# Block inverses of the recurrent stage: VectorE's 32x32 transposition and level products 32 columns wide

## The chip, the core and the metric

The kernel runs on one core of one Trainium2 chip. The metric is device time in microseconds (us) for one launch, lower is better. TensorE (PE in the profile) multiplies matrices: it loads a stationary operand (PEld, a weight load) and streams a moving operand past it, into PSUM. VectorE (DVE), ScalarE (ACT) and GpSimd (POOL) work elementwise. Each engine runs its own instruction stream in order and waits for the others by semaphores.

## The reference

Two transformer-like blocks are computed one after the other for 512 tokens of 1024 channels. The first has a feed-forward network, a mixer of three branches and a second feed-forward network. The second has a bidirectional recurrence (RWKV-7), a neighbourhood attention, a merge, and a mixture of 16 experts. Only the recurrence bears on this case. It has 8 heads of 64 channels, two directions, first 256 context tokens and then 512 latent tokens:

```python
def rwkv_scan(s0, r, decay, k, v, kk, a, reverse, emit):
    def step(s, inp):
        w_t, k_t, v_t, kk_t, a_t = inp[:5]
        s_kk = jnp.einsum('bhvk,bhk->bhv', s, kk_t)
        s = (s * w_t[:, :, None, :]
             - s_kk[..., None] * (kk_t * a_t)[:, :, None, :]
             + v_t[..., None] * k_t[:, :, None, :])
        y = jnp.einsum('bhvk,bhk->bhv', s, inp[5]) if emit else None
        return s, y
...
    for d in range(2):
...
        s_c, yc_d = rwkv_scan(s0, r_c, w_c, kd_c, v_c, kk_c, a_c, rev, emit_ctx)
        w_x, kd_x, a_x = dir_x[d]
        _, yx_d = rwkv_scan(s_c, r_x, w_x, kd_x, v_x, kk_x, a_x, rev, True)
```

## The kernel before

**Chunks.** The recurrence is not run token by token. It goes over 12 chunks (`NCH`) of 64 tokens (`L`): chunks 0 to 3 are context and emit nothing, chunks 4 to 11 emit outputs (`emits`). Both directions are done together. A "tile" is 64x64; a chunk has 8 tiles of one kind (`ALL`): 4 for direction 0 (`LOW`), 4 for direction 1 (`HIGH`). Each tile holds two heads, one in partitions 0 to 63, one in 64 to 127. `tiles` (L1978) issues one matmul per head, so two per tile, all at L1983. A product `ALONG` keeps a head in its own half of partitions, one `ACROSS` lands in the other half.

**What a chunk needs.** Inside a chunk the delta rule needs the inverse X of a unit triangular 64x64 matrix per head and direction, made from the pair product A = kappa x b. The pair products are `AT` (transposed), `A`, `CT`, `R1`, `R2`, and the transposes `kT`, `bT`, `vt`, which are matmuls against the identity. The state products are G, U, Z and y. The `lora_pe` matmuls (L2019) make decays for the chunk after next.

**The inverse by levels.** `XX[c % 2]` holds X and its transpose XT side by side for each direction. ScalarE writes identities there (`unit`, L1908, 128x1024). VectorE then copies the neighbour elements of AT into XT and of A into X under a mask (`pair_XT`, `pair_X`, each a `copy_predicated`, L2273). From there five levels l = 1 to 5 join blocks of 2^l into blocks of 2^(l+1). Each level has four steps for each direction d:

- PE: Y = A times X, 4 tiles of 64 columns (`level_Y`).
- DVE: `Ym` = Y times the level's mask, 128x256 (`level_y`, L2291).
- PE: W = X times Ym into the X half of a PSUM bank, and its transpose into the XT half, 8 tiles (`level_W`); at level 5 only the transposed one, 4 tiles.
- DVE: XX += W, 128x512, at level 5 128x256 (`level_x`, L2299).

**The order.** It is written out by hand. On PE the loop over chunks interleaves each level product with another product that is ready (`beside`, tile by tile), such as the next chunk's pair products or the last chunk's state products; `alone` issues one kind only. On VectorE the loop puts other work between the masked products and the additions: the scaled keys of the next chunk after `level_y` of level 1, the decay logits of the chunk after next at level 2, `pair_XT` and a scan at level 3, `pair_X` after `level_x` of level 3, the state addition (L2305), the CT mask (L2286) and a key product at level 4, the state decay (L2311) and a scan before level 5. Every wait is on a semaphore whose value a table of names gives (`Marks`, `Steps`).

A "full" chunk window, as the prediction uses it, is one in which the next chunk emits and the chunk after next still needs its decays: 496 matmuls.

Of the kernel before, what the change touches and what calls it, by code (L numbers as in the profile page):

```python
# [14 lines left out]
P = 128  # L15
# [83 lines left out]
def hybrid_block_kernel(nc, stream, par, x_t, mod_w, c_rows, vbias, gate_w, masks, ctx_t, rpb, router_w, lora, experts, spill, gates_dram, xs_dram, ys_dram, out):  # L99
    ctx = ExitStack()  # L100
    with ctx:
# [447 lines left out]
        hz_ready = sem("hgrn_zeros")  # L549
# [4 lines left out]
        zero_ready = sem("zero_ready")  # L554
# [13 lines left out]
        def hgrn_pool(pool):  # L568
            pool.dma_start(vb, vbias).then_inc(vb_in, 16)
            pool.memset(zero_row[:, :], 0.0).then_inc(zero_ready, 1)  # L570
            pool.wait_ge(zero_ready, 1)
# [6 lines left out]
            pool.memset(ql, 0.0).then_inc(hz_ready, 1)  # L578
            pool.memset(kl, 0.0).then_inc(hz_ready, 1)
# [204 lines left out]
        def hgrn_dve(dve):  # L784
# [43 lines left out]
            def head(h):  # L828
# [13 lines left out]
                if h == 0:  # L842
                    dve.wait_ge(hz_ready, 2)
# [76 lines left out]
        l_zero = sem("lru_zeros")  # L920
# [6 lines left out]
        def lru_pool(pool):  # L927
            pool.wait_ge(hv.sem, hv.end(HEADS))
            pool.memset(lxp[:, 0:3], 0.0).then_inc(l_zero, 1)
            pool.memset(acc_odd[:, 0:1], 0.0).then_inc(l_zero, 1)  # L930
# [56 lines left out]
        def lru_act(act):  # L987
            s = la.sem
            act.sem_inc(s, la.base)
            act.wait_ge(l_zero, 2)  # L990
# [63 lines left out]
        def lru_dve(dve):  # L1054
            s = lv.sem
            dve.sem_inc(s, lv.base)
            dve.wait_ge(l_zero, 2)
# [689 lines left out]
        Ym, Gs, Us = take(W8, "a"), take(W8, "a"), take(W8, "a")  # L1747
        yacc = take(8 * 4 * L, "a").rearrange("p (c q v) -> p c q v", c=8, q=4)
# [24 lines left out]
        M_BANK = dict(vt=6, AT=4, A=5, CT=6, kT=4, bT=5, R1=6, R2=4)  # L1773
# [18 lines left out]
        pe_m = Marks("rwkv_pe_pairs", lambda c: ("AT", "A", "CT", "kT", "bT") + (("R1", "R2") if emits(c) else ()) + ("vt",))  # L1792
# [8 lines left out]
        dve_l = Marks("rwkv_dve_levels", lambda c: [f"{n}{l}{d}" for l in LV for n in ("ym", "x") for d in range(2)])  # L1801
# [7 lines left out]
        rz = sem("rwkv_zeros")  # L1809
# [18 lines left out]
        def rwkv_pool(pool):  # L1828
# [3 lines left out]
            pool.memset(st[0], 0.0).then_inc(rz, 1)  # L1832
            pool.memset(reset, 1.0).then_inc(rz, 1)
            pool.wait_ge(rz, 2)
            pool.memset(bd(reset)[:, :, 0:1], 0.0).then_inc(rz, 1)
# [44 lines left out]
        def rwkv_act(act):  # L1880
# [90 lines left out]
        def rwkv_pe(pe):  # L1971
# [6 lines left out]
            def tiles(n, bank, *terms, start=None, at=None):  # L1978
# [12 lines left out]
            ALL, LOW, HIGH = range(8), range(4), range(4, 8)  # L1991

# [39 lines left out]
            def pair_A(c):  # L2032
                if c:
                    W(act_m, c - 1, "bT")
                return lambda n: tiles(n, M_BANK["A"], (ACROSS, of(kap[c % 3]), of(bt)))

# [10 lines left out]
            def pair_bT(c):  # L2047
                W(dve_m, c, "X")
                return lambda n: tiles(n, M_BANK["bT"], (ACROSS, of(bt), eye))

# [14 lines left out]
            def level_Y(c, l, d):  # L2065
                if l == 1:
                    W(act_m, c, "AT")
                    W(dve_m, c, "X")
                    if c:
                        W(dve_l, c - 1, f"x5{d}")  # L2070
                else:
                    W(dve_l, c, f"x{l - 1}{d}")
                return lambda n: tiles(n, d, (ALONG, of(AT[c % 2]), X_of(c)), at=n % 4 * L)

            def level_W(c, l, d):
                W(dve_l, c, f"ym{l}{d}")

                def one(n):
# [58 lines left out]
            pe.wait_ge(rz, 3)  # L2137
            pe.wait_ge(kn_dve.sem, kn_dve.end(1))
            alone(pair_AT(0), ALL, pe_m)
            alone(pair_A(0), ALL, pe_m)  # L2140
# [4 lines left out]
            for c in range(NCH):  # L2145
# [9 lines left out]
                w = level_W(c, 1, 0)  # L2155
                beside(w, ALL, pe_l, pair_vt(c), ALL, pe_m)
                alone(level_W(c, 1, 1), ALL, pe_l)
# [4 lines left out]
                if more:  # L2162
                    beside(w, ALL, pe_l, pair_AT(n), ALL, pe_m)
                    w = level_W(c, 2, 1)
                    beside(w, ALL, pe_l, pair_A(n), ALL, pe_m)
                    level_Ys(c, 3, pair_CT(n), pe_m)
                else:
                    alone(w, ALL, pe_l)
                    alone(level_W(c, 2, 1), ALL, pe_l)
                    level_Ys(c, 3)  # L2170
                w = level_W(c, 3, 0)
                if last:
                    z = state_Z(s)
                    beside(w, ALL, pe_l, z, LOW)
                    w = level_W(c, 3, 1)
                    beside(w, ALL, pe_l, z, HIGH, pe_s)
                else:
                    alone(w, ALL, pe_l)
                    alone(level_W(c, 3, 1), ALL, pe_l)
# [5 lines left out]
                if y:  # L2185
                    beside(w, ALL, pe_l, state_y_old(s), ALL, pe_s)
                    alone(state_y_new(s), ALL, pe_s)
                else:
                    alone(w, ALL, pe_l)
                w = level_W(c, 4, 1)  # L2190
                if more:
                    beside(w, ALL, pe_l, pair_bT(n), ALL, pe_m)
                else:
                    alone(w, ALL, pe_l)
# [4 lines left out]
                if r:  # L2199
                    other = pair_R2(n)  # L2200
                    w = level_W(c, 5, 0)
                    beside(w, HIGH, pe_l, other, LOW)
                    w = level_W(c, 5, 1)
                    beside(w, HIGH, pe_l, other, HIGH, pe_m)
                else:
                    alone(level_W(c, 5, 0), HIGH, pe_l)
                    alone(level_W(c, 5, 1), HIGH, pe_l)
# [8 lines left out]
        def rwkv_dve(dve):  # L2216
# [70 lines left out]

            def level_y(c, l):
                for d in range(2):
                    wait(pe_l, c, f"Y{l}{d}")  # L2290
                    dve.tensor_tensor(half(Ym, d), bd(psum[:, d, 0:4 * L]), m4(M_LOW + l, d), ALU.mult).then_inc(dve_l.sem, 1)  # L2291

            def level_x(c, l):
                for d in range(2):
                    wait(pe_l, c, f"W{l}{d}")
                    wait(dve_m, c, "X") if l == 1 else wait(dve_l, c, f"x{l - 1}{d}")
# [46 lines left out]
            dve.wait_ge(rz, 3)  # L2343
# [77 lines left out]
        xz = sem("ybd_zero")  # L2421
# [43 lines left out]
        def rwkv_out_dve(dve):  # L2465
# [21 lines left out]
            dve.wait_ge(xz, 2)  # L2487
# [14 lines left out]
        def rwkv_out_pool(pool):  # L2502
            pool.wait_ge(dve_s.sem, dve_s.end())
            pool.dma_start(gate_a[:, :, :], gates_dram[:, 0::2, :]).then_inc(gates_in[0], 16)
            for n in range(2):
                pool.memset(ybd[n], 0.0).then_inc(xz, 1)
# [150 lines left out]
        tri_ready = sem("tri_ready")  # L2657
# [113 lines left out]
        def moe_pool(pool):  # L2771
            pool.wait_ge(ye.sem, 4)
            pool.dma_start(rw, router_w).then_inc(router_in, 16)
            pool.memset(tri, 1.0).then_inc(tri_ready, 1)
            pool.wait_ge(tri_ready, 1)
            pool.affine_select(out=tri, in_=tri, compare_op=ALU.is_ge, fill=0.0, base=-1,
                               pattern=[[1, P]], channel_multiplier=-1).then_inc(tri_ready, 1)
# [55 lines left out]
        def moe_pe(pe):  # L2833
# [18 lines left out]
            pe.wait_ge(tri_ready, 2)  # L2852
# [489 lines left out]
```

## Time and profile before

| what | value |
|---|---|
| median of 3 runs | 3183.29 us (3182.76 to 3189.88) |
| profiled execution: span from first to last instruction | 3176.4 us |
| what lies around the span, median minus span | 6.9 us |
| PE busy | 2844.9 us, 90% |
| DVE busy | 1810.3 us, 57% |
| ACT busy | 1423.0 us, 45% |
| POOL busy | 862.1 us, 27% |
| recurrent stage, first level product to its end | 2177 to 2516 us |
| granted PE clock over the span | 0.957 |

The granted clock is a share of 2.4 GHz. The profiled execution's own time is given as its span; the runs' times are a little longer, by the last difference in the table. Profile and views name instructions by line, engine, operation and tiles; "mem", "shared", "resid" and "zero_row" are large buffers in which the stage's tiles lie. An fp32 matmul of this stage shows as two records of PE and two weight loads.

### The profile page before, as it was taken

To read this page: it belongs to the slowest core of one execution; us is meant where nothing else is said; L and a number is where in the kernel's file an instruction comes from. 1 tells how busy PE (TensorE), PEld (TensorE's weight loads), DVE (VectorE), ACT (ScalarE), POOL (GpSimd) and SP (SyncE) were. 2 spreads that over 40 slices of the span, in tenths; PEclk is the share of its full clock that TensorE was granted. 3 is DMA by queue.
4 is the path that set the end of the run, shared out by engine and by line. 5 is a ranking of instruction groups with operands and counts; after the bars stand their busy time and mean duration, and the time that the engine had idled before them with its cause. 6 is when DMAs were issued, how large, how long until landed. Compare 5 with 4: busy or idle time off the path is not lost. (4 is left out here: it accounts for less than half of the span.)

```text
span 3176.4 us, 56806 instructions
## 1 busy us (share of the span) xinstructions
PE 2844.9 (90%) x22816; PEld 2316.8 (73%) x22816; DVE 1810.3 (57%) x2643; ACT 1423.0 (45%) x1914; POOL 862.1 (27%) x519
## 2 busy tenths in 40 slices
PE   7999989898899899899997999996777678699996
PEld 5887868776678687788775787776777566588884
DVE  3115556888999742311446303447766554599996
ACT  4435444555652332434444223335333123488884
POOL 4444452220015343344432233322222031000001
PEclk9999999999999999999998999998999879899997
DMA  3325552112223132233542122221000023799996
GB/s 110 96 96 179 189 222 66 47 60 65 84 76 96 64 125 84 76 99 96 202 159 96 54 86 70 82 74 33 4 5 4 29 73 114 285 411 412 412 412 248
DMA packets 109959, 412.50 MB, mean 130 GB/s; under 512 B 12016, under 2 KB 12032, under 8 KB 108752
## 3 DMA queue, kind: packets, MB, share of 16 engines
q1 hardware_dynamic: 88128, 322.24, 28.8%
q0 software_dynamic: 11136, 48.26, 4.1%
q10 hardware_dynamic: 10512, 39.33, 3.5%
q8 instruction: 144, 2.36, 0.3%
q14 instruction: 39, 0.32, 0.0%
HBM read 370.45 MB, written 39.32 MB: 129 GB/s over the span
## 5 line engine op out<-in xcount | busy, mean ns | idle before, releaser
L214 POOL TENSOR_TENSOR ring_r<-ring,whi 128x1024 fp32r<-128x1024 f32 x243 | 598.2, 2472 | 1001.6 <-ACT whi L209 1001.5
L226 PE MATMUL psum<-xn_r,whi 128*128 128x512 f32 x1208 | 474.4, 393 | 0.0
L209 ACT ACTIVATE whi<-ring 128x1024 fp32r<-128x1024 f32 x247 | 255.7, 1054 | 424.4 <-DMA ring<-stream 424.1
L224 PE MATMUL psum<-xh,ring_r 128*128 128x512 f32 x952 | 396.4, 416 | 38.3 <-DVE ring_r L214 20.1
L1983 PE MATMUL psum<-mem 64*64 64x64 f32 x9664 | 250.7, 224 | 82.9 <-issue 32.3
L2757 DVE TENSOR_TENSOR er_r<-er,eh 128x1024 fp32r<-128x1024 f32 x268 | 309.7, 1219 | 1.0 <-ACT eh L2746 0.4
L1983 PEld LDWEIGHTS psum<-mem 64*64 64x64 f32 x9664 | 230.8, 137 | 102.0 <-issue 68.2
L224 PE MATMUL psum<-ffn_xh,ring_r 128*128 128x512 f32 x704 | 276.6, 393 | 17.7 <-DVE xn_r L237 17.7
L2746 ACT ACTIVATE eh<-er 128x1024 fp32r<-128x1024 f32 x268 | 268.5, 1071 | 41.9 <-DMA er<-experts 40.5
L225 PE MATMUL psum<-ffn_xh,whi 128*128 128x512 f32 x704 | 275.7, 392 | 0.0
L226 PEld LDWEIGHTS psum<-xn_r,whi 128*128 128x128 f32 x1208 | 229.1, 190 | 49.0
L224 PEld LDWEIGHTS psum<-xh,ring_r 128*128 128x128 f32 x952 | 181.9, 191 | 98.9 <-DVE ring_r L214 23.5
L518 DVE TENSOR_TENSOR gu<-gu,psum 128x512 f32<-128x512 f32 x44 | 30.3, 688 | 344.6 <-ACT gu L499 344.6
L225 PE MATMUL psum<-xh,whi 128*128 128x512 f32 x504 | 198.9, 395 | 0.0
L226 PE MATMUL psum<-xn_r,whi_h 128*128 128x512 f32 x448 | 177.6, 397 | 0.0
L225 PE MATMUL psum<-xh,whi_h 128*128 128x512 f32 x448 | 177.5, 396 | 0.0
L439 DVE TENSOR_TENSOR mem<-mem 128x1024 f32<-128x1024 f32 x64 | 129.5, 2052 | 70.3 <-ACT mem L421 65.9
L224 PEld LDWEIGHTS psum<-ffn_xh,ring_r 128*128 128x128 f32 x704 | 133.0, 189 | 49.7 <-POOL ring_r L214 18.7
L225 PEld LDWEIGHTS psum<-ffn_xh,whi 128*128 128x128 f32 x704 | 133.3, 189 | 26.7
L224 PE MATMUL psum<-hid_hi,ring_r 128*128 (+1 forms) x352 | 144.6, 411 | 8.5 <-DVE hid_lo L522 7.6
L2817 PE MATMUL psum<-er_r,xbh 128*128 128x512 f32 x368 | 147.0, 399 | 3.4 <-DVE er_r L2757 2.0
L214 POOL TENSOR_TENSOR ring_r<-ring,whi_h 128x1024 fp32r<-128x1024 f32 x36 | 90.4, 2536 | 209.0 <-ACT whi_h L209 209.0
(510 smaller groups left out, 6033.4 us busy)
## 6 DMA issues: line engine op xcount, KB each, us to landing
ring<-stream SPq DMA_DIRECT2D x311, 512.0 KB, 3.5
er<-experts SPq DMA_DIRECT2D x276, 512.0 KB, 8.4
mem<-mod_w ACTq DMA_DIRECT2D x48, 512.0 KB, 4.1
xs_dram<-zero_row POOLq DMA_DIRECT2D x1, 12288.0 KB, 39.2
xs<-xs_dram SPq DMA_DIRECT2D x23, 512.0 KB, 8.3
ys_dram<-y_t ACTq DMA_DIRECT2D x23, 512.0 KB, 6.5
spill<-resid POOLq DMA_DIRECT2D x2, 2048.0 KB, 10.8
resid<-spill POOLq DMA_DIRECT2D x2, 2048.0 KB, 8.6
```

What stands on the lines that cost most here:

```text
L209: act.activation(WHI.get(part, whi)[:, (SLAB_AT[part] + j) % RING, :, :], w, ACT.Copy).then_inc(w_hi, 1)
L214: pool.tensor_tensor(ring_r[:, s, :, :], ring[:, s, :, :], f(WHI.get(part, whi)[:, s, :, :]), ALU.subtract).then_inc(w_lo, 1)
L224: pe.matmul(bank, lo[:, b, :], x_hi_, start=start, stop=False, skip_group_check=True)
L225: pe.matmul(bank, hi[:, b, :], x_hi_, start=False, stop=False, skip_group_check=True)
L226: return pe.matmul(bank, hi[:, b, :], x_lo_, start=False, stop=stop, skip_group_check=True)
L439: dve.tensor_tensor(mod_t[at % 2], mod_wb[m % 4], mod_c[:, s, :], ALU.mult).then_inc(mod_mul, 1)
L518: dve.tensor_tensor(gu[:, half, :], gu[:, half, :], psum[:, 2 * half, :], ALU.mult).then_inc(sg_ready, 1)
L1983: ins = pe.matmul(psum[o, bank, first:first + L], lhs(n)[r], rhs(n)[r], start=i == 0 if start is None else start, stop=i == len(terms) - 1 ...
L2746: act.activation(eh[:, SLOT[kind] + j, :], er[:, SLOT[kind] + j, :], ACT.Copy).then_inc(e_hi, 1)
L2757: dve.tensor_tensor(er_r[:, at, :], er[:, at, :], f(eh[:, at, :]), ALU.subtract).then_inc(e_lo_dve, 1)
L2817: pe.matmul(bank, x_hi_, lo_[:, cols], start=start, stop=False, skip_group_check=True)
```

## The change

1. **A is dropped.** `pair_A`, its mark and its PSUM bank go. `pair_X` no longer copies under a mask; VectorE transposes XT's four-by-four grid of 32x32 blocks into X in one instruction (128x512). Up to level 4 an inverse has nothing outside its 32x32 diagonal blocks. `unit` writes identities only into XT.
2. **Transposed inverses of levels 1 to 4** are made by VectorE: after the two additions of a level, one transposition of 128x256 for each direction (`t{l}{d}`). `level_W` makes only the X half, so 4 tiles instead of 8. Level 5 makes only the XT half, as before, without a transposition.
3. **Level products are 32 columns wide.** Level l changes only every second group of 2^l columns. `level_Y` streams those 32 columns of X, `level_y` writes them packed into a new buffer `Yc` (at level 5 into `Ym`, filled with zeros once), `level_W` streams 32 columns, `level_x` adds into the strided places. VectorE's operations on them become 128x128.
4. **PE's order** follows: W of levels 1 to 4 has 4 tiles per direction; `vt` and the next `AT` are spread over both directions of levels 1 and 2. `bT` waits for ScalarE's copy of the last chunk instead of for X.
5. **Fills on one semaphore.** GpSimd's memsets in the whole kernel count on `filled` with a table `FILLS`, in the same order.

```diff
-        M_BANK = dict(vt=6, AT=4, A=5, CT=6, kT=4, bT=5, R1=6, R2=4)
+        M_BANK = dict(vt=6, AT=4, CT=6, kT=4, bT=5, R1=6, R2=4)
...
-                eye = two_ident.unsqueeze(1).to_broadcast([P, 16, L])
-                act.activation(XX[c % 2].rearrange("p (n t) -> p n t", n=16), eye, ACT.Copy).then_inc(act_m.sem, 1)
+                eye = two_ident.unsqueeze(1).unsqueeze(1).to_broadcast([P, 2, 4, L])
+                act.activation(XX[c % 2].rearrange("p (d w q t) -> p d w q t", d=2, w=2, q=4)[:, :, 1, :, :], eye, ACT.Copy).then_inc(act_m.sem, 1)
...
-                        ins = pe.matmul(psum[o, bank, first:first + L], lhs(n)[r], rhs(n)[r],
+                        ins = pe.matmul(psum[o, bank, first:first + wide], lhs(n)[r], rhs(n)[r],
...
+            turned_half = lambda tile, l, h: tile.rearrange("p (b h t) -> p b h t", h=2, t=2 ** l)[:, :, h, :]
...
-                return lambda n: tiles(n, d, (ALONG, of(AT[c % 2]), X_of(c)), at=n % 4 * L)
+                changed = lambda n: turned_half(X_of(c)(n), l, d)
+                return lambda n: tiles(n, d, (ALONG, of(AT[c % 2]), changed), at=n % 4 * 32, wide=32)
...
                 def one(n):
-                    if n >= 4:
-                        return tiles(4 * d + n - 4, d, (ALONG, of(Ym), XT_of(c)), at=n * L)
-                    return tiles(4 * d + n, d, (ALONG, XT_of(c), of(Ym)), at=n * L)
+                    if l == 5:
+                        return tiles(4 * d + n, d, (ALONG, of(Ym), last_rows), at=n * 32, wide=32)
+                    return tiles(4 * d + n, d, (ALONG, XT_of(c), product), at=n * 32, wide=32)
...
-                beside(w, ALL, pe_l, pair_vt(c), ALL, pe_m)
-                alone(level_W(c, 1, 1), ALL, pe_l)
+                v = pair_vt(c)
+                beside(level_W(c, 1, 0), LOW, pe_l, v, LOW)
+                beside(level_W(c, 1, 1), LOW, pe_l, v, HIGH, pe_m)
...
-                wait(pe_m, c, "A")
                 wait(dve_m, c, "XT")
-                chosen(c, 0, M_BANK["A"], M_LOW)
+                dve.transpose(xx(c)[:, :, 0, :, :], xx(c)[:, :, 1, :, :]).then_inc(dve_m.sem, 1)
...
-                    dve.tensor_tensor(half(Ym, d), bd(psum[:, d, 0:4 * L]), m4(M_LOW + l, d), ALU.mult).then_inc(dve_l.sem, 1)
+                    to = blocks(half(Ym, d), l, d) if l == 5 else packed(Yc[:, 2 * L * d:2 * L * (d + 1)], l)
+                    dve.tensor_tensor(to, packed(psum[:, d, 0:2 * L], l), blocks(m4(M_LOW + l, d), l, d), ALU.mult).then_inc(dve_l.sem, 1)
...
-                    first = 4 * L if l == 5 else 0
-                    then = XX[c % 2][:, W8 * d + first:W8 * (d + 1)]
-                    dve.tensor_tensor(then, then, psum[:, d, first:W8], ALU.add).then_inc(dve_l.sem, 1)
+                    whole = xx(c)[:, d, 1 if l == 5 else 0, :, :]
+                    then = blocks(whole, l, 1 - d if l == 5 else d)
+                    dve.tensor_tensor(then, then, packed(psum[:, d, 0:2 * L], l), ALU.add).then_inc(dve_l.sem, 1)
+                if l < 5:
+                    for d in range(2):
+                        wait(dve_l, c, f"x{l}{d}")
+                        dve.transpose(xx(c)[:, d, 1, :, :], xx(c)[:, d, 0, :, :]).then_inc(dve_l.sem, 1)
```

How the order on PE changes, in the middle of a full chunk: the state product U (16 matmuls), then W of level 2 beside the next chunk's pair products. Before:

```order
L1983 MATMUL psum<-mem 64x64 [waits rwkv_act_state,rwkv_dve_levels]
L1983 MATMUL psum<-mem 64x64 x15
L1983 MATMUL psum<-mem 64x64 [waits rwkv_pool_decay,rwkv_dve_decay,rwkv_dve_pairs,rwkv_dve_levels]
L1983 MATMUL psum<-mem 64x64 x31
L1983 MATMUL psum<-mem 64x64 [waits rwkv_act_pairs,rwkv_dve_levels]
L1983 MATMUL psum<-mem 64x64 x31
```

And of the change, from the same place on:

```order
L1983 MATMUL psum<-mem 64x64 [waits rwkv_act_state,rwkv_dve_levels]
L1983 MATMUL psum<-mem 64x64 x15
L1983 MATMUL psum<-mem 64x32 [waits rwkv_pool_decay,rwkv_dve_decay,rwkv_dve_pairs,rwkv_dve_levels]
L1983 MATMUL psum<-mem 64x32
L1983 MATMUL psum<-mem 64x64 x2
L1983 MATMUL psum<-mem 64x32 x2
L1983 MATMUL psum<-mem 64x64 x2
L1983 MATMUL psum<-mem 64x32 x2
L1983 MATMUL psum<-mem 64x64 x2
L1983 MATMUL psum<-mem 64x32 x2
L1983 MATMUL psum<-mem 64x64 x2
L1983 MATMUL psum<-mem 64x32 [waits rwkv_dve_levels]
```

U stands as before; the two runs of 32 matmuls each (W beside AT, W beside A) have become two of 16, of which the first and the start of the second are shown, half of them with 32 columns.

How the order on VectorE changes, from the masked products of level 3 to those of level 4 and the state addition. Before:

```order
L2291 TENSOR_TENSOR mem<-psum,shared 128x256 [waits rwkv_pe_levels] x2
L2272 MEMSET tick 128x1 [waits rwkv_act_pairs]
L2273 COPY_PREDICATED mem<-shared,psum 128x2x256
L2248 SCALAR_TENSOR_TENSOR resid<-mem,zero_row 128x256 [waits rwkv_pool_decay,rwkv_act_decay]
L2299 TENSOR_TENSOR mem<-mem,psum 128x512 [waits rwkv_dve_levels,rwkv_pe_levels] x2
L2272 MEMSET tick 128x1 [waits rwkv_dve_pairs,rwkv_pe_pairs]
L2273 COPY_PREDICATED mem<-shared,psum 128x2x256
L2291 TENSOR_TENSOR mem<-psum,shared 128x256 [waits rwkv_pe_levels] x2
L2305 TENSOR_TENSOR mem<-mem,psum 128x512 [waits rwkv_pe_state]
```

And of the change:

```order
L2297 TENSOR_TENSOR mem<-psum,shared 128x128 [waits rwkv_pe_levels] x2
L2273 MEMSET tick 128x1 [waits rwkv_act_pairs]
L2274 COPY_PREDICATED mem<-shared,psum 128x2x256
L2249 SCALAR_TENSOR_TENSOR resid<-mem,zero_row 128x256 [waits rwkv_pool_decay,rwkv_act_decay]
L2305 TENSOR_TENSOR mem<-mem,psum 128x16x8 [waits rwkv_dve_levels,rwkv_pe_levels] x2
L2309 STREAM_TRANSPOSE mem<-mem 128x256 [waits rwkv_dve_levels] x2
L2282 STREAM_TRANSPOSE mem<-mem 128x2x256 [waits rwkv_dve_pairs]
L2297 TENSOR_TENSOR mem<-psum,shared 128x128 [waits rwkv_pe_levels] x2
L2315 TENSOR_TENSOR mem<-mem,psum 128x512 [waits rwkv_pe_state]
```

The additions are a quarter as large and followed by two transpositions, and X comes from a transposition instead of a second predicated copy with its small memset.

## Rows read from the trace of the kernel before

**Rows 1.** The page's busy row of PE; the line view of L1983.

```profile
PE 2844.9 (90%) x22816; PEld 2316.8 (73%) x22816; DVE 1810.3 (57%) x2643; ACT 1423.0 (45%) x1914; POOL 862.1 (27%) x519
...
L1983 PE MATMUL psum<-mem x9664: 212/219/366, 2161.6 to 2516.1; 64*64 64x64 f32 x198
...
L1983 PE MATMUL psum<-shared,mem x1152: 213/218/366, 2167.9 to 2487.0; 64*64 64x64 f32 x192
```

**Rows 2.** Windows: us; busy us (x instructions) of PE, PEld, DVE, ACT, POOL; clock; DMA; GB/s.

```profile
2177.00:2516.00 339.00, 265.85 (x10939) 246.01 (x10941) 218.27 (x462) 106.75 (x207) 74.36 (x99) 0.98 0.02 4
2222.30:2248.10 25.80, 20.20 (x832) 18.70 (x832) 18.31 (x41) 9.62 (x19) 6.11 (x8) 1.00 0.02 4
2248.10:2272.70 24.60, 20.54 (x848) 18.88 (x848) 18.59 (x40) 9.67 (x20) 7.50 (x10) 1.00 0.02 5
...
2300.50:2330.00 29.50, 23.30 (x992) 21.19 (x992) 19.27 (x43) 10.31 (x22) 7.49 (x10) 1.00 0.02 5
2330.00:2360.20 30.20, 22.73 (x992) 21.10 (x992) 19.23 (x43) 10.35 (x22) 7.48 (x10) 1.00 0.02 5
2360.20:2388.60 28.40, 22.70 (x992) 21.02 (x992) 19.16 (x43) 10.38 (x22) 7.48 (x10) 1.00 0.02 4
```

**Rows 3.** Timeline of PE: start us, duration us, records, idle before and its releaser.

```profile
2263.07 2.66 PE L1983 MATMUL psum<-mem 64*64 64x64 f32 x127 [0.90 <-issue]
2266.46 1.16 PE L1983 MATMUL psum<-mem 64*64 64x64 f32 x48 [0.72 <-issue]
...
2347.38 2.68 PE L1983 MATMUL psum<-mem 64*64 64x64 f32 x127 [1.10 <-issue]
2351.26 1.03 PE L1983 MATMUL psum<-mem 64*64 64x64 f32 x41 [1.20 <-issue]
```

**Rows 4.** DMA queues, 2177 to 2516 us: packets, MB, share of 16 engines.

```profile
q8 instruction: 86, 1.41, 1.8%
```

**Rows 5.** Waits of PE and PEld, 2177 to 2516 us: total us, times, longest.

```profile
PE psum L1983 <- issue: 34.8, 42, 1.5
PE psum L1983 <- DVE mem L2299: 12.5, 36, 1.1
PE psum L1983 <- DVE mem L2305: 7.7, 7, 1.3
...
PE psum L1983 <- DVE mem L2291: 5.9, 12, 0.9
PE psum L1983 <- DVE mem L2318: 5.2, 3, 2.1
...
PEld psum L1983 <- issue: 58.4, 84, 1.7
```

**Rows 6.** Timeline of PE: alternating products, then one kind alone.

```profile
2256.16 0.23 PE L1983 MATMUL psum<-mem 64*64 64x64 f32 x2
2256.18 0.23 PE L1983 MATMUL psum<-shared,mem 64*64 64x64 f32 x2
2256.22 0.23 PE L1983 MATMUL psum<-mem 64*64 64x64 f32 x2
...
2256.40 1.64 PE L1983 MATMUL psum<-mem 64*64 64x64 f32 x48
```

**Rows 7.** Timeline of DVE: two operations back to back.

```profile
2331.20 0.73 DVE L2291 TENSOR_TENSOR mem<-psum,shared 128x256 f32<-128x256 f32 x2
...
2343.35 1.28 DVE L2236 TENSOR_TENSOR zero_row<-psum,mem 128x512 f32<-128x512 f32 x2
```

**Rows 8.** Groups of DVE in the stage: count, busy us, mean ns, idle before.

```profile
L2299 DVE TENSOR_TENSOR mem<-mem,psum 128x512 f32<-128x512 f32 x96 | 65.6, 686 | 84.6 <-PE psum L1983 84.3
L2291 DVE TENSOR_TENSOR mem<-psum,shared 128x256 f32<-128x256 f32 x118 | 48.0, 419 | 26.6 <-PE psum L1983 26.0
...
L2273 DVE COPY_PREDICATED mem<-shared,psum 128x512 f32<-128x512 uint32 x22 | 16.1, 731 | 0.0
```

**Rows 9.** Windows as in rows 2, where the clock is below 1.

```profile
2450.00:2460.00 10.00, 7.37 (x274) 7.04 (x274) 7.35 (x19) 1.94 (x5) 4.99 (x7) 0.83 0.03 5
2516.00:2600.00 84.00, 51.57 (x188) 37.69 (x184) 48.92 (x58) 22.22 (x34) 22.49 (x15) 0.67 0.21 69
```

More of the change, by code:

```diff
@@ L548, in hybrid_block_kernel @@
         hv_done = sem("hgrn_values")
-        hz_ready = sem("hgrn_zeros")
+        filled = sem("pool_fills")
+        FILLS = {"zero_row": 1, "levels": 3, "lru": 5, "state": 7, "reset": 8, "last_level": 9, "ybd": 11, "tri_ones": 12, "tri": 13}
         vb_in = sem("vb_in")
@@ L569, in hgrn_pool @@
             pool.dma_start(vb, vbias).then_inc(vb_in, 16)
-            pool.memset(zero_row[:, :], 0.0).then_inc(zero_ready, 1)
-            pool.wait_ge(zero_ready, 1)
+            pool.memset(zero_row[:, :], 0.0).then_inc(filled, 1)
+            pool.wait_ge(filled, FILLS["zero_row"])
             pool.dma_start(xs_dram.rearrange("(b p) d -> p b d", p=P),
@@ L577, in hgrn_pool @@
             pool.dma_start(spill, resid[:, :, :]).then_inc(mix_spilled, 16)
-            pool.memset(ql, 0.0).then_inc(hz_ready, 1)
-            pool.memset(kl, 0.0).then_inc(hz_ready, 1)
+            pool.memset(ql, 0.0).then_inc(filled, 1)
+            pool.memset(kl, 0.0).then_inc(filled, 1)
             for g in range(2):
@@ L842, in head @@
                 if h == 0:
-                    dve.wait_ge(hz_ready, 2)
+                    dve.wait_ge(filled, FILLS["levels"])
                 for li, L in enumerate(LEVELS):
@@ L928, in lru_pool @@
             pool.wait_ge(hv.sem, hv.end(HEADS))
-            pool.memset(lxp[:, 0:3], 0.0).then_inc(l_zero, 1)
-            pool.memset(acc_odd[:, 0:1], 0.0).then_inc(l_zero, 1)
+            pool.memset(lxp[:, 0:3], 0.0).then_inc(filled, 1)
+            pool.memset(acc_odd[:, 0:1], 0.0).then_inc(filled, 1)
             with pool.Fori(0, DT) as j:
@@ L1747, in hybrid_block_kernel @@
         Ym, Gs, Us = take(W8, "a"), take(W8, "a"), take(W8, "a")
+        Yc = take(4 * L, "b")
         yacc = take(8 * 4 * L, "a").rearrange("p (c q v) -> p c q v", c=8, q=4)
@@ L1800, in hybrid_block_kernel @@
         dve_m = Marks("rwkv_dve_pairs", lambda c: ("XT", "X", "CT", "R1", "R2") if emits(c) else ("XT", "X", "CT"))
-        dve_l = Marks("rwkv_dve_levels", lambda c: [f"{n}{l}{d}" for l in LV for n in ("ym", "x") for d in range(2)])
+        dve_l = Marks("rwkv_dve_levels", lambda c: [f"{n}{l}{d}" for l in LV for n in ("ym", "x") + (("t",) if l < 5 else ()) for d in range(2)])
         dve_s = Marks("rwkv_dve_state", lambda c: (("z", "zz") if c + 1 < NCH else ()) + (("y0", "y1") if second_sum(c) else ()))
@@ L1831, in rwkv_pool @@
             pool.wait_ge(na_d.sem, na_d.end())
[L1832 to L1835, printed above, removed]
+            pool.memset(st[0], 0.0).then_inc(filled, 1)
+            pool.memset(reset, 1.0).then_inc(filled, 1)
+            pool.wait_ge(filled, FILLS["state"])
+            pool.memset(bd(reset)[:, :, 0:1], 0.0).then_inc(filled, 1)
+            pool.memset(Ym, 0.0).then_inc(filled, 1)
             for n in range(2):
@@ L1976, in rwkv_pe, with tiles @@
             ACROSS, ALONG = 1, 0
-            def tiles(n, bank, *terms, start=None, at=None):
+            def tiles(n, bank, *terms, start=None, at=None, wide=L):
                 first = n * L if at is None else at
@@ L2162, in rwkv_pe @@
                 if more:
[L2163 removed]
+                    a = pair_AT(n)
+                    beside(w, LOW, pe_l, a, LOW)
                     w = level_W(c, 2, 1)
[L2165 removed]
+                    beside(w, LOW, pe_l, a, HIGH, pe_m)
                     level_Ys(c, 3, pair_CT(n), pe_m)
                 else:
[L2168 to L2169 removed]
+                    alone(w, LOW, pe_l)
+                    alone(level_W(c, 2, 1), LOW, pe_l)
                     level_Ys(c, 3)
@@ L2173, in rwkv_pe @@
                     z = state_Z(s)
-                    beside(w, ALL, pe_l, z, LOW)
+                    beside(w, LOW, pe_l, z, LOW)
                     w = level_W(c, 3, 1)
-                    beside(w, ALL, pe_l, z, HIGH, pe_s)
+                    beside(w, LOW, pe_l, z, HIGH, pe_s)
                 else:
-                    alone(w, ALL, pe_l)
-                    alone(level_W(c, 3, 1), ALL, pe_l)
+                    alone(w, LOW, pe_l)
+                    alone(level_W(c, 3, 1), LOW, pe_l)
                 if more:
@@ L2201, in rwkv_pe @@
                     w = level_W(c, 5, 0)
-                    beside(w, HIGH, pe_l, other, LOW)
+                    beside(w, LOW, pe_l, other, LOW)
                     w = level_W(c, 5, 1)
-                    beside(w, HIGH, pe_l, other, HIGH, pe_m)
+                    beside(w, LOW, pe_l, other, HIGH, pe_m)
                 else:
-                    alone(level_W(c, 5, 0), HIGH, pe_l)
-                    alone(level_W(c, 5, 1), HIGH, pe_l)
+                    alone(level_W(c, 5, 0), LOW, pe_l)
+                    alone(level_W(c, 5, 1), LOW, pe_l)
             s = NCH - 1
@@ L2286, in masked @@
                 dve.tensor_tensor(both(dst[c % 2]), P8(M_BANK[name]), m8(n), ALU.mult).then_inc(dve_m.sem, 1)
+            blocks = lambda v, l, h: v.rearrange("p q (b h t) -> p q b h t", h=2, t=2 ** l)[:, :, :, h, :]
+            packed = lambda v, l: v.rearrange("p (q b t) -> p q b t", q=4, t=2 ** l)
             def level_y(c, l):
@@ L2505, in rwkv_out_pool @@
             for n in range(2):
-                pool.memset(ybd[n], 0.0).then_inc(xz, 1)
+                pool.memset(ybd[n], 0.0).then_inc(filled, 1)
         merged2 = mem[:, 0:DT * T].rearrange("p (m t) -> p m t", t=T)
```

48 lines of the change are left out of this document (21 added, 27 removed).

## Prediction

> **What bounds the kernel now.** I read first the page's busy shares: TensorE (PE) is busy for 90% of the span, so it is the engine to follow. The change touches only the recurrent stage, which I find by its line: all matmuls of L1983 start between 2161 and 2516 us [rows 1]. The windows by chunk come second [rows 2]. From the first level product at 2177 to 2516 us there are 339 us, with 10939 matmul records. One `pe.matmul` leaves two records (the program has 5408 at L1983, the trace 10816), and each has a weight load of its own. The other windows are chunks, each from one decay of the state (L2311) to the next. A full chunk has 992 records and takes 28.4 to 30.2 us. PE is busy for only 22.7 to 23.3 us of that, VectorE (DVE) for 19.2. So what fills the rest?
>
> The timeline of PE answers it [rows 3]. Where no other engine is waited for, PE runs 127 records in 2.7 us and then stands still for 0.7 to 1.2 us, put down to "issue", that is to nothing the profile shows. With their loads 127 records are some 254 instructions. The queue table shows 86 packets of code in the stage (1.41 MB, so 16 KB each), one per 254 instructions [rows 4]. The starts of such runs lie 3.39 us (2263.07 to 2266.46) and 3.88 us (2347.38 to 2351.26) apart, mean 3.6 us. At 3.6 us, 86 blocks of code are 310 of the 339 us. The table of waits closes the sum: PE waited for DVE 12.5 + 7.7 + 5.9 + 5.2 = 31 us, for "issue" 34.8 us, and its weight loads 58.4 us for "issue" [rows 5]. So the stage goes by the number of PE instructions, at 3.6 us per 127 records, plus some 29 us of waits that no code fetch covers.
>
> Here a rule speaks against this reading. The Trainium skill, Runtime: NRT & Kernel Launch, section Instruction fetch mechanics, says that code is refilled in 16 KiB blocks of 256 instructions and that crossing a boundary is mostly hidden. The block size agrees with the packets; the hiding does not agree with the idle times behind each 127 records. By that rule instructions that go would be worth only their streaming time; that is rival B, priced from rows.
>
> **Records removed.** The untransposed product A goes: 16 matmuls in each of 12 chunks. The level products of levels 1 to 4 no longer make the transposed inverse: 2 directions x 4 tiles x 2 = 16 matmuls in each of 4 levels and 12 chunks. Together 192 + 768 = 960 matmuls or 1920 records (5408 to 4448 in the built program). A chunk loses 160: 992 becomes 832, 832 becomes 672. The price per record I take from windows of different size [rows 2]: the three full windows average 29.4 us for 992 records, the two early ones 25.2 us for 840: 4.2 us per 152 records, 27.6 ns each. 1920 x 27.6 ns = 53 us. By blocks it is 1920 / 127 = 15 blocks x 3.6 = 54 us. First term: **-53 us**.
>
> **Narrower products.** 1920 of the 4448 remaining matmuls have 32 moving columns rather than 64. No such row exists. A run that uses two quarters of the array takes (1.64 - 0.23) / 48 = 29 ns per record, one that alternates with products crossing the halves takes 0.058 us for four, 14.5 ns [rows 6]. Most narrow products alternate with 64-column ones, whose own pace stays, and PE waits for code anyway. Only the level 2 products stand alone; at 14.5 ns instead of 29 their 32 records would give 0.46 us a chunk, 5 us in all. Bounds 0 to -5; I take 0, since the nearest rows are the alternating ones.
>
> **VectorE's work.** Back to back, two 128x256 operations end 0.73 us after the first start and two of 128x512 1.28 us after it; one alone takes 0.42 and 0.68 us [rows 7, 8]. So an extra one costs about 0.37 and 0.64 us, hence 0.27 us per 256 elements and 0.10 fixed, and a 128x128 one 0.24 us. Per chunk: eight additions shrink from 0.64 to 0.24 (-3.2), two from 0.37 to 0.24 (-0.3), ten masked products from 0.37 to 0.24 (-1.3), the predicated copy for X becomes one transposition of the same size (-0.1, with its memset). Eight transpositions of 128x256 come in. None is in this trace: a floor is 0.24 us (a smaller operation), a ceiling twice the full one, 0.8. I take the 128x256 row with 0.01 more, 0.38: +3.0. Net -1.9 us of DVE per chunk, 19.2 becoming 17.3. The Trainium skill, VectorE: DVE Perf Modes, section The three transpose paths, gives 311 ns for a 128x128 transposition in bf16; with the slope above that makes 0.44 us for 128x256 alone, an estimate, and the sum would be -41 us by it.
>
> What counts is where it lies. The two transpositions of a level stand between its additions and the next masked products, while PE does the next Y. By place, in a full chunk (DVE needs against PE's cover, at 0.93 us for 64 alternating records): from x2 to y3 1.06 against 0.93 becomes 1.29 against 0.93 (+0.2); from x4 to y5, behind the state decay and a scan, 1.70 against 0.47 becomes 2.33 (+0.6); from y2 to x2, where PE has half as many products left, 2.34 against 1.86 becomes 1.80 against 0.93 (+0.4); from y3 to x3 the wait of 0.6 nearly goes (-0.5); y5 to x5 -0.25; the last addition of level 4 -0.4; x3 to y4 +0.15. Sum +0.2 us a chunk, **+2 us**.
>
> **Waits that the code fetch hid.** Summed in the same way, a full chunk has some 6.6 us of DVE waits, 72 us over 11 chunks, of which 29 to 31 show [rows 5]; 42 lie inside stalls for code. With 15 stalls fewer (86 to 71) I let the hidden part fall in proportion, 42 x 71 / 86 = 35: **+7 us**. Early chunks would have DVE busy 16.5 of 21 us, fuller than any window now; for that **+2 us**. Bounds of both together 0 to +30.
>
> Edits at nothing: ScalarE's unit copy halves from 1024 to 512 elements a row, but ScalarE is busy only 10 of 30 us [rows 2]; the gathering of fills on one semaphore keeps their order on GpSimd; the extra fill of `Ym` is 0.5 us before the stage, covered by PE's lora products. bT no longer waits for X but for ScalarE's copy of the last chunk, long done.
>
> Sum: -53 + 2 + 7 + 2 = **-42 us**. The profiled execution has a span of 3176.4 us; the median of the runs is 6.9 us above it. 3183.3 - 42 = **3141.3 us**.
>
> **Rivals.** B, code isn't the bound and only PE's streaming counts: a chunk loses two times 0.93 us (levels 1 and 2; at 3 and 4 the partner products keep their length), 1.9 x 11.5 = 22 us: 3161. For it: DVE is waited for in 31 us. Against: the regular 127. Chance 0.11. C, more than forecast: waits stay hidden and narrow runs quicken, 53 + 5 and less DVE: 3124. For it: DVE has less work; against: PE covers less. 0.15. D, a transposition costs 0.8 us: 8 x 0.4 = 3.2 us a chunk, all between x and y: +37, 3178, no measurable change. 0.06. E, **slower**: PE's clock. The granted clock is 1.00 in nearly all of the stage, but 0.83 in 2450 to 2460 us, after waits, and 0.67 in the thinner stretch behind 2516 [rows 9]. With half the columns in 320 of 832 records, PE does less. PE's busy 22.9 us of a full chunk less the 1.9 of rival B, less some 0.2 us of run-out after each of about 15 runs of records, leave 18 us of streaming; at 1.2 GHz they take 18 more, 200 us over 11 chunks: from 21% of the stage at that level the gain is gone; at 40% it is 3141 + 80 = 3221. Against it: records per us barely change (33 now, 32 to 33 after). 0.05. F, the rest of small outcomes around no change (the level chain turning out longer at several of the places above, +35): 3176. 0.05.
>
> **Numbers.** Forecast 3141 (own range 3128 to 3155), chance 0.58; C 0.15, B 0.11, D 0.06, F 0.05, E 0.05. From 3120 (C with all waits hidden) to 3171 (B with half the waits given back) leaves out most of D, E and F and a little of C: 0.8 inside. A measurement of this kernel can tell about 0.3% (9.5 us) from no change. Faster: 0.58 + 0.15 + 0.11 + a little of D and F = 0.86; same 0.08; slower 0.06.
>
> **What would show it.** Stage from about 339 to 297 us; some 71 packets of code; runs of 127 records still followed by "issue" idle times near 1 us; full chunks 25 to 26 us and early ones 21 to 22; transpositions of 128x256 near 0.43 us each in the list of groups; PE's waits for DVE at 35 to 45 us. The prediction is wrong if "issue" stays as large with fewer packets, if DVE's transpositions take over 0.6 us, or if the granted clock of the stage falls under 0.95.

## Result and profile after

The changed kernel takes 3138.2 us (median of 4 runs, 3133.7 to 3145.5), before 3186.6 us: a ratio of 0.9853, 95% interval 0.9835 to 0.9870, so about 48 us less. Measured again beside others it was 0.9861 (0.9844 to 0.9878). The forecast was 3141.3 us. One execution of the kernel before in a later series took 11815 us and counts in none of the ratios.

The page of the changed kernel, span and busy shares; then the windows, read as [rows 2]: the stage, an early chunk, the one before the full ones, and three full ones.

```profile
span 3135.8 us, 53029 instructions
PE 2818.7 (90%) x20896; PEld 2296.9 (73%) x20896; DVE 1781.0 (57%) x2727; ACT 1417.9 (45%) x1914; POOL 865.9 (28%) x520
```

```profile
2172.00:2475.80 303.80, 242.08 (x9054) 227.75 (x9056) 192.77 (x547) 101.67 (x207) 77.08 (x99) 0.90 0.02 4
2207.90:2233.50 25.60, 22.29 (x678) 21.15 (x675) 16.10 (x48) 9.02 (x19) 6.50 (x8) 0.73 0.02 4
...
2255.40:2276.70 21.30, 16.89 (x743) 15.77 (x736) 17.51 (x49) 9.33 (x20) 7.48 (x10) 1.00 0.02 4
2276.70:2301.80 25.10, 19.69 (x834) 18.25 (x826) 17.19 (x49) 9.89 (x22) 7.50 (x10) 1.00 0.02 5
2301.80:2333.50 31.70, 25.74 (x856) 24.36 (x859) 17.39 (x49) 9.85 (x22) 7.89 (x10) 0.78 0.02 4
2360.90:2385.90 25.00, 19.48 (x845) 18.13 (x840) 17.36 (x50) 9.79 (x22) 7.89 (x10) 1.00 0.02 5
```

PE has 1920 instructions less than in [rows 1], as counted. The stage takes 303.8 us against 339 in [rows 2]; what follows it is 660 us in both profiles, and the remaining 5 us lie ahead of the stage, which begins at 2172 instead of 2177 us; in another profiled execution of the kernel before, it began at 2173.0. Full chunks at clock 1.00 take 25.0 to 25.1 us; the one at 0.78 takes 31.7, and an early one at 0.73 takes 25.6. This is new: every chunk shown in [rows 2] had 1.00. In a second profiled execution of the changed kernel both early chunks ran at 1.00; they took 20.7 us on average, where [rows 2] has 25.2:

```profile
2210.50:2231.40 20.90, 16.29 (x674) 15.19 (x672) 15.86 (x47) 8.84 (x19) 6.10 (x8) 1.00 0.02 5
2231.40:2251.90 20.50, 16.67 (x708) 15.66 (x709) 16.51 (x48) 9.48 (x20) 8.09 (x10) 1.00 0.02 5
```

The timeline of PE (as [rows 3]), the code queue (as [rows 4]) and PE's waits (as [rows 5]) of the changed kernel:

```profile
2291.10 2.76 PE L1983 MATMUL psum<-mem 64*64 64x32 f32 x127 [1.11 <-issue]
2294.85 0.24 PE L1983 MATMUL psum<-mem 64*64 64x32 f32 x2 [0.99 <-issue]
```

```profile
q8 instruction: 71, 1.16, 1.7%
```

```profile
PE psum L1983 <- issue: 24.0, 28, 1.6
PE psum L1983 <- DVE mem L2297: 14.0, 18, 1.2
PE psum L1983 <- DVE mem L2315: 8.4, 7, 1.6
PE psum L1983 <- DVE mem L2328: 4.7, 3, 2.0
PE psum L1983 <- DVE mem L2305: 3.7, 7, 0.8
```

A run of 127 records in 2.76 us still stands between idle times of 1.0 to 1.1 us. The starts lie 3.75 us apart (2291.10 to 2294.85), within the prediction's 3.39 to 3.88. 71 packets of code came, as forecast; that number only says that the instructions are fewer. With waits, a full chunk at clock 1.00 takes 3.8 us per run of 127 (25.05 us for 832 records, or 6.55 runs), and before it took the same 3.8 (29.4 us for 992). The waits for VectorE are 14.0 + 8.4 + 4.7 + 3.7 = 31 us, where [rows 5] had 31.

The timeline of VectorE with two operations back to back (as [rows 7]), and its groups in the stage (as [rows 8]):

```profile
2286.42 0.76 DVE L2309 STREAM_TRANSPOSE mem<-mem 128x256 f32<-128x256 f32 x2
2287.22 0.48 DVE L2297 TENSOR_TENSOR mem<-psum,shared 128x128 f32<-128x128 f32 x2
```

```profile
L2309 DVE STREAM_TRANSPOSE mem<-mem 128x256 f32<-128x256 f32 x96 | 36.6, 420 | 0.0
L2305 DVE TENSOR_TENSOR mem<-mem,psum 128x128 f32<-128x128 f32 x120 | 33.1, 283 | 87.2 <-PE psum L1983 86.2
L2297 DVE TENSOR_TENSOR mem<-psum,shared 128x128 f32<-128x128 f32 x118 | 30.3, 278 | 15.4 <-PE psum L1983 14.9
```

Two transpositions in 0.76 us are 0.38 us each, two narrow products in 0.48 us are 0.24 each: both to the digit what the forecast put together. The recorded duration of one transposition is 0.42 us. The estimate from the 311 ns that the Trainium skill (VectorE: DVE Perf Modes, section The three transpose paths) gives for 128x128 in bf16 was 0.44.

PE's narrow products of one kind alone (level 2), to set against the last row of [rows 6]:

```profile
2286.10 1.12 PE L1983 MATMUL psum<-mem 64*64 64x32 f32 x32
```

The 32 records of Y at level 2 take (1.12 - 0.23) / 31 = 29 ns each, just as with 64 columns. Half the columns quicken nothing on PE here, and the zero taken for them was right even where the forecast allowed 5 us.

### The profile page after: what moved, and what is told of

Read it like the earlier page. It is cut to its first block and busy times, and to the rows that moved or that the text cites. A ratio compares the mean times of both kernels' runs of the same rounds, so it can differ in the third digit from the quotient of the medians.

```text
span 3135.8 us, 53029 instructions
## 1 busy us (share of the span) xinstructions
PE 2818.7 (90%) x20896; PEld 2296.9 (73%) x20896; DVE 1781.0 (57%) x2727; ACT 1417.9 (45%) x1914; POOL 865.9 (28%) x520
## 5 line engine op out<-in xcount | busy, mean ns | idle before, releaser
L1983 PE MATMUL psum<-mem 64*64 64x64 f32 (+1 forms) x7744 | 219.1, 231 | 70.1 <-issue 20.4
L1983 PEld LDWEIGHTS psum<-mem 64*64 64x64 f32 x7744 | 203.9, 145 | 84.5 <-issue 56.8
```

Source lines behind the costliest of these rows:

```text
L1983: ins = pe.matmul(psum[o, bank, first:first + wide], lhs(n)[r], rhs(n)[r], start=i == 0 if start is None else start, stop=i == len(terms) ...
```

## Experiments

Time is given as ratio to the kernel before, whose median in each of the two timed series was 3181.7 us.

### Instructions put back: is it their number or their time on the array?

The 768 matmuls that the change had taken from levels 1 to 4 came back as copies into a part of PSUM that nobody reads, 32 or 2 columns wide; everything on VectorE stayed as in the changed kernel. For 32, with one of the calls that now issue them:

```diff
                 def one(n):
                     if l == 5:
                         return tiles(4 * d + n, d, (ALONG, of(Ym), last_rows), at=n * 32, wide=32)
+                    if n >= 4:
+                        extra = lambda m: Yc[:, m * 32:m * 32 + 32]
+                        return tiles(4 * d + n - 4, d, (ALONG, XT_of(c), extra), at=n * 32, wide=32)
                     return tiles(4 * d + n, d, (ALONG, XT_of(c), product), at=n * 32, wide=32)
...
-                beside(level_W(c, 1, 0), LOW, pe_l, v, LOW)
+                beside(level_W(c, 1, 0), ALL, pe_l, v, LOW)
```

> The changed kernel with the 768 matmuls of levels 1 to 4 put back as copies of the narrow W product whose results nobody reads (32 columns, 1536 records more). VectorE's work is unchanged. Theory fetch (the pace is set by instructions, 27.6 ns per record): +42 us against the changed kernel, about 3180, and 83 packets of code in the stage. Theory streaming (only time on the array counts, 14.5 ns per alternating record or less): +11 to +22 us, 3149 to 3160.

> As the run with 768 matmuls put back, but each of them streams 2 columns instead of 32. Theory fetch: the width is of no account, the same time as with 32 columns within 5 us, about 3180. Theory streaming: the 2-column matmuls are nearly free, 3138 to 3148.

Measured: 32 columns 0.9989 (0.9971 to 1.0007), 2 columns 1.0006 (0.9987 to 1.0026). The ratio rises by 0.013 to 0.015 over the changed kernel, 41 to 49 us, or 27 to 32 ns a record. Stage windows (as [rows 2]) with 32 and with 2 columns, the code queue and the group of 2-column matmuls of the latter:

```profile
2174.60:2520.20 345.60, 282.04 (x10590) 267.99 (x10592) 194.30 (x547) 103.19 (x207) 74.57 (x99) 0.88 0.02 4
2173.50:2517.20 343.70, 280.28 (x10592) 267.20 (x10592) 194.64 (x547) 103.18 (x207) 74.59 (x99) 0.89 0.02 4
```

```profile
q8 instruction: 83, 1.36, 1.6%
...
L1983 PE MATMUL psum<-mem 64*64 64x2 f32 x1536 | 65.1, 200 | 4.3 <-issue 4.3
```

Both stages take within 2 us of each other. 1536 records more are 12 packets of code more (83 against 71), and about 44 us more of stage (341 us, the mean of these two and of one more with 32 columns below, against 297, the mean of three profiled executions of the changed kernel): 3.7 us a packet, 29 ns a record. A matmul of 2 columns costs what one of 32 does. So what counts is the number of instructions, and theory streaming, rival B, falls.

The copies alone don't tell a wait for code from a fixed time that PE takes for each instruction. The times of the code packets in the traces do. In the stage of the kernel before, PE stood still 32 times for over 0.5 us with the reason "issue", and each time it went on 1.2 to 1.6 us after a code packet had landed. In the changed kernel there were 21 such pauses, each ending 1.2 to 1.7 us after a landing; with copies of 2 columns 29, 1.2 to 1.5 us. PE's long waits for other engines show no such tie: they end anywhere from 0 to over 5 us after a landing. So these pauses end with the arrival of code. The Trainium skill (Runtime: NRT & Kernel Launch, section Instruction fetch mechanics) states blocks of 16 KiB, which agrees with 1.36 MB in 83 packets; that crossing into the next block is mostly hidden does not agree with this stream of small matmuls.

### One part alone: A dropped

In the kernel before, `pair_A` goes, X comes from one transposition, and `bT` waits as in the changed kernel. The edit for X:

```diff
             def pair_X(c):
-                wait(pe_m, c, "A")
                 wait(dve_m, c, "XT")
-                chosen(c, 0, M_BANK["A"], M_LOW)
+                dve.transpose(xx(c)[:, :, 0, :, :], xx(c)[:, :, 1, :, :]).then_inc(dve_m.sem, 1)
```

> One part of the change alone, on the kernel before: A is dropped and X comes from a transposition of XT; everything else as before. 192 matmuls or 384 records less: at 27.6 ns each -10.6 us against before, at the full share of a stall for each 127 records -11. If the records under W of level 2 were covered by VectorE's work anyway: -2 to -4. Slower than before is excluded by either.

Measured: 0.9961 (0.9945 to 0.9976), 12 us less (8 to 17). So 384 records less give 32 ns each (20 to 46), and this part is a quarter of the gain with a fifth of the records. The price per record fits, within a wide interval.

### Transpositions twice: how much of VectorE's chain shows?

```diff
                     for d in range(2):
                         wait(dve_l, c, f"x{l}{d}")
+                        if c or l > 1:
+                            wait(dve_l, c if l > 1 else c - 1, f"s{l - 1 if l > 1 else 4}{d}")
+                        dve.transpose(half(spare, d), xx(c)[:, d, 0, :, :]).then_inc(dve_l.sem, 1)
+                    for d in range(2):
                         dve.transpose(xx(c)[:, d, 1, :, :], xx(c)[:, d, 0, :, :]).then_inc(dve_l.sem, 1)
```

> The changed kernel with each of the 96 transpositions of levels 1 to 4 done twice, first into a spare buffer that nobody reads. In the changed kernel's profile one of 128x256 takes 0.42 us alone. If VectorE's chain between the additions and the next masked product sets the pace there, 8 x 0.37 us a chunk show fully: +35 us, 3173. If stalls for code cover it, as the prediction took for most of the waits, about 40% shows: +14 us, 3152. If VectorE's work here is covered altogether: under +5 us.

Measured: 0.9922 (0.9897 to 0.9947), 19 to 22 us slower than the changed kernel by the two ratios measured for that one, with an interval of some 10 us to either side. The stage (as [rows 2]), one place on VectorE (as [rows 7]) and PE's waits (lines shifted by one to five):

```profile
2174.90:2497.90 323.00, 249.88 (x9055) 234.29 (x9056) 220.59 (x643) 102.73 (x207) 74.63 (x99) 0.87 0.02 4
```

```profile
2285.61 0.76 DVE L2312 STREAM_TRANSPOSE mem<-mem 128x256 f32<-128x256 f32 x2
2286.30 0.73 DVE L2314 STREAM_TRANSPOSE mem<-mem 128x256 f32<-128x256 f32 x2
```

```profile
PE psum L1984 <- DVE mem L2298: 29.0, 27, 1.8
PE psum L1984 <- issue: 13.5, 18, 1.5
PE psum L1984 <- DVE mem L2320: 10.9, 7, 2.2
PE psum L1984 <- DVE mem L2306: 8.7, 17, 0.6
PE psum L1984 <- DVE mem L2333: 4.7, 3, 2.0
```

PE's waits for VectorE rise from 31 to 53 us, its idle times for "issue" fall from 24.0 to 13.5: a wait first takes the place of a stall for code and only then lengthens the stage. That is the covering which the forecast reckoned with. How much it covers stays open. Two transpositions start 0.69 us before the next two, so 96 more are 33 us of VectorE's stream (its busy time in the stage rose by 28 us, from 192.8 to 220.6), and 19 to 22 us of longer runs would be more than half of that. But the interval is wide, and part of the time is the clock, 0.87 here against 0.90 to 0.94.

### The clock: columns or something else?

The changed kernel's stage had 0.90 of the clock, before's 0.98. Is it the missing columns? First, level products 64 columns wide again in the changed kernel, with unchanged counts and waits (the buffer and VectorE's addresses follow, not shown):

```diff
-                return lambda n: tiles(n, d, (ALONG, of(AT[c % 2]), changed), at=n % 4 * 32, wide=32)
+                return lambda n: tiles(n, d, (ALONG, of(AT[c % 2]), X_of(c)), at=n % 4 * L)
...
-                    return tiles(4 * d + n, d, (ALONG, XT_of(c), product), at=n * 32, wide=32)
+                    return tiles(4 * d + n, d, (ALONG, XT_of(c), product), at=n * L)
```

> The changed kernel, but the level products of levels 1 to 4, and Y of level 5, stream 64 columns again (a 128x512 buffer takes the place of the packed one, zeroed once; the 32 columns that a level doesn't change are computed and not used). Number of matmuls (4448), waits and VectorE's operations (128x128) stay. In the changed kernel's profile the granted clock of the stage is 0.90 where before's was 0.98, and full chunks at clock 1.00 take 25.0 us, others up to 31.7. Theory A (the clock falls because half the columns of the level products are gone): the stage's clock comes back to 0.96 or more, the stage takes 285 to 290 us rather than 303, and the kernel about 3122. Theory B (the clock falls because of PE's idle times between the runs, which stay): clock about 0.90, stage 303 us or a few more, kernel 3138 to 3145.

> The changed kernel with level products that stream 64 columns, again, for an interval against the changed kernel. Theory A (columns keep the clock up): 8 to 12 us faster than the changed kernel on the same chip. Theory B (the first difference came from chip or chance): within 4 us of it.

> The changed kernel as it is, on the same chip as the three below. Ratio to before 0.984 to 0.988; granted clock of the stage 0.88 to 0.92 again if the fall belongs to the kernel and not to one execution.

The first time it gave 0.9843 (0.9820 to 0.9867), a time near what theory A said, but with a stage clock of 0.93 instead of 0.96 or more. In one series with the changed kernel it was 0.9858 (0.9841 to 0.9875) against 0.9861 (0.9844 to 0.9878): no difference. Then the same width with the 768 unread copies put back, and one more profiled execution each of four kernels:

> The kernel with 64-column level products and the 768 matmuls of levels 1 to 4 put back as unread copies, 64 columns wide. It has the instructions and waits of the run with 32-column copies (stage clock 0.87 to 0.9, some 3179 us), only more columns. Theory A (columns decide the clock): stage clock 0.96 or more, and a time at least 10 us under that run, about 3165. Theory B (idle times decide): stage clock as low and 3175 to 3185.

> The kernel before, for a second look at the granted clock of its stage. In its profile the stage (first level product to last, 339 us) spent 15 us at 1.2 GHz. If the clock's falls belong to the change: 10 to 25 us again. If they vary as much with every execution: anything up to 60.

> The changed kernel, third look. The first two had 61 and 40 us of the stage at 1.2 GHz and stages of 304 and 293 us. Theory: 40 to 60 us again, and a stage of 273 us plus half of what it spends at 1.2 GHz.

> The changed kernel with 768 unread copies of the narrow W product (32 columns), second look. First look: 82 us at 1.2 GHz; with copies of 2 columns 79 us. Theory A (columns decide): 70 to 90 again. Theory B (chance or idle times): about 40 as with 64 columns.

> The same instructions and waits with 64 columns in all level products and copies, second look. First look: 41 us at 1.2 GHz. Theory A: 30 to 50 again, well under the 32-column kernel. Theory B: as much as that one.

Stage windows (as [rows 2]), the granted clock being the third number from the end. The kernel before, second execution; the changed kernel, second and third; with 64 columns, both:

```profile
2173.00:2516.90 343.90, 266.37 (x10943) 245.70 (x10944) 218.51 (x463) 106.72 (x207) 74.48 (x99) 0.98 0.02 4
2174.60:2467.90 293.30, 231.58 (x9054) 217.09 (x9056) 192.32 (x547) 101.76 (x207) 76.44 (x99) 0.93 0.02 4
2169.80:2464.20 294.40, 231.65 (x9056) 216.87 (x9056) 191.52 (x547) 101.98 (x207) 76.23 (x99) 0.94 0.02 4
2171.00:2467.00 296.00, 234.90 (x9056) 218.54 (x9056) 193.42 (x547) 102.17 (x207) 76.53 (x99) 0.93 0.02 4
2171.10:2468.30 297.20, 234.51 (x9056) 218.24 (x9056) 192.89 (x547) 101.95 (x207) 76.83 (x99) 0.94 0.02 4
```

With 32-column copies, second execution; with 64-column copies, both; A alone dropped:

```profile
2176.10:2510.20 334.10, 262.45 (x10591) 247.28 (x10592) 194.46 (x547) 103.15 (x207) 74.65 (x99) 0.97 0.02 4
2174.30:2513.10 338.80, 271.19 (x10591) 254.47 (x10592) 193.88 (x547) 103.18 (x207) 74.64 (x99) 0.94 0.02 4
2173.00:2514.40 341.40, 273.69 (x10590) 257.78 (x10592) 193.94 (x547) 103.17 (x207) 74.58 (x99) 0.92 0.02 4
2174.50:2506.20 331.70, 267.52 (x10590) 247.48 (x10592) 217.27 (x452) 106.77 (x207) 74.51 (x99) 0.97 0.02 4
```

The copies of 64 columns took 0.9980 (0.9969 to 0.9992), not told apart from those of 32. The clock with 32-column copies was 0.88 and then 0.97, with 64-column ones 0.94 and 0.92. So in single profiles the clock scatters from one execution to the next more than with the width. None of the four second looks settled it: the kernel with 32-column copies spent some 20 us at the lower level, less than either theory had said. What does hold is that kernels with before's level arithmetic had 0.97 to 0.98 (three executions, of two kernels) and those with the changed one 0.87 to 0.97 (eleven, of which one above 0.94).

The timed executions say more, since each has a granted clock over the whole span (the stage is a tenth of it). Their means:

| kernel | executions | mean clock of the span |
|---|---|---|
| before, either series | 18 and 17 | 0.956 |
| A alone dropped | 6 | 0.955 |
| copies of 64 columns | 10 | 0.951 |
| copies of 32 columns | 10 | 0.949 |
| copies of 2 columns | 10 | 0.944 |
| changed kernel, in the series of the result and in a later one | 4 and 4 | 0.948 and 0.951 |
| changed with 64 columns, in an earlier series and in that later one | 4 and 4 | 0.954 and 0.952 |

Copies of 32 and of 2 columns ran in one series and scatter by 0.003 each, so their difference of 0.0045 is clear of the noise: fewer columns did lower the clock there. In the changed kernel itself it isn't clear: 0.001 between the two widths within the later series, 0.006 between the two other ones, which are not the same series. The larger part of the fall is something else: the kernel without A and the one with 64-column copies have the same number of records in the stage (10590 and 10591) and nearly the same columns, and still 0.955 against 0.951. They differ in VectorE's level operations and in the order on PE; which of these matters stays open. In time the latter is slower by 0.0019, 6 us (0 to 12), so at an equal number of instructions VectorE's smaller operations and transpositions brought no gain that these runs show. The lower clock may account for the difference.

What a fall costs can be read from one kernel: the changed kernel's stage took 303.8 us at 0.90, 293.3 at 0.93 and 294.4 at 0.94. A clock of 0.90 is 61 us at the lower of the two levels (1.2 of 2.4 GHz), 0.93 is 41, 0.94 is 35. 20 us more at the lower level were 10.5 us more stage, 26 us more were 9.4: some 0.35 to 0.5 us per us. Chunks of one execution agree: the full one at 0.78 had 13.9 us at the lower level and took 6.6 us more than those at 1.00. It isn't a constant, though. The kernel with 32-column copies took 345.6 us at 0.88 and 334.1 at 0.97, 11.5 us for 63 us, 0.2 us per us; and before's stage took 339.0 and 343.9 us at the same 0.98.

## Why the prediction was right, and where it wasn't

**The bound.** "One packet of code per 127 records, 3.6 us each": confirmed by the copies of 2 columns, which cost as much as those of 32, by the pauses, which all end 1.2 to 1.7 us after a code packet has landed, and by the pace at clock 1.00 (3.8 us with waits, before and after). This step carried the forecast.

**The first term, -53 us.** Right in size. The full chunks at clock 1.00 went from 29.4 us (mean of three in [rows 2]) to 25.0, -4.4, as 160 x 27.6 ns had it; early ones went from 25.2 to 20.7. The price per record was found again at 27 to 32 ns.

**VectorE's durations** were right to 0.01 us, its stage sum went from 218.3 to 192.8 us, -25.5, where -1.9 a chunk had made -23. No run shows that this shortened the stage.

**The waits, +2 +7 +2 us.** This step failed. It let the waits that stalls had covered come out as stalls became fewer; PE's waits for VectorE should have grown from 31 us to between 35 and 45. They stayed at 31 us, and at 31 and 28 in the other two executions. That the cover is finite is right (the doubled transpositions drove them to 53 us), but 15 stalls fewer took nothing measurable from it. A likely reason, not tested alone, is that VectorE's own work shrank with PE's. The early chunks, reckoned the tightest, ran at 20.9 and 20.5 us at clock 1.00, under the 21 to 22 forecast, so the +2 for them did not come either.

**The clock.** It was put at zero in the sum and kept as rival E. One of the prediction's own signs of being wrong, a granted clock of the stage under 0.95, came in all three profiled executions of the changed kernel. The changed stage spent 35 to 61 us at the lower level, 12 to 20% of it, before's 14 us (0.98 of 339). At 0.35 to 0.5 us each, the 21 to 47 us more took back 7 to 23 us. So the rival's mechanism was there, short of deciding, and happened to fill the place of the waits that did not come; that is luck. Its price, 200 us on a stage that would then last some 500 or 0.4 us per us, lies within the 0.2 to 0.5 measured. Its reason, half the columns, is the smaller part at most: fewer columns lowered the clock in the copies, but 64 columns did not bring before's clock back.

**The sum.** -42 us forecast, 47 to 48 measured in medians; in profiled spans -40.6 us, with the clock at its lowest of the three executions, and -53 us between the third (3124.3) and before's second (3177.3). The chunks at clock 1.00 alone, 4.4 and 4.5 us less over some 11.5 chunks, would make about -51. The forecast stands 6 us off because two terms of about 10 us, waits that did not come and a clock put at zero, nearly cancelled.

**The rivals.** B fell with the copies. C is what the chunks at clock 1.00 resemble: waits hidden as before, though without any gain from narrowness. D fell: a transposition takes 0.42 us, not 0.8. None of the tried variants beats the changed kernel beyond the intervals.

## What to carry to other kernels

Where a stage consists of many small matmuls, set the regular idle times of TensorE beside the packets of its code: if a pause comes behind every 127 records and ends at much the same time after a packet has landed, an instruction is the unit of cost, and work should move to whichever engine needs fewer of them, however little each streams. Narrowing a matmul then buys nothing on TensorE. It makes the operations on the engine that reads the result smaller, but no gain from that could be shown here. And an estimate from one profile should carry the granted clock of the stage as a term with its own spread: here it moved the same kernel by 10 us.

## What the runs showed of the hardware that was not expected

- A 64x64 matmul of 2 columns in fp32 costs as much wall time in such a stream as one of 32: 343.7 against 345.6 us of stage, at the same number of instructions.
- Each pause of PE over 0.5 us put down to "issue" ended 1.2 to 1.7 us after a 16 KB packet of code had landed (32 pauses before, 21 after).
- Of one kind alone, products of 32 columns follow each other at 29 ns per record, as do those of 64.
- The granted clock of a stage that is 80% busy varied from 0.90 to 0.94 between executions of one binary and from 0.88 to 0.97 of another. With unread copies of 2 columns instead of 32 the mean clock of the whole span was 0.944 instead of 0.949 (ten executions each).
- VectorE's 32x32 transposition of 128x256 fp32 elements costs 0.38 us back to back, what a masked product of that size does (0.37).
